# Hybrid decoder block with routed experts: whole weight rows with k outermost, and the expert's second row block in 32-row column groups in fp32

## What is computed

```
logits = xt @ w_router + b_router;  top_vals, top_idx = top_k(logits, 4);  gates = softmax(top_vals)
gu  = xb @ w_gu[e] + b_gu[e]        # w_gu[e]: 1024 x 2048
g   = min(gu[:, :1024], 7);  up = clip(gu[:, 1024:], -7, 7)
y   = ((up + 1) * g * sigmoid(1.702 * g)) @ w_down[e] + b_down[e]    # w_down[e]: 1024 x 1024
out[token] += gate * y              # then a last RMSNorm
```

## Time and profile before

| | |
|---|---|
| median of 3 runs | 2089.41 us (2071.77, 2089.41, 2090.12) |
| the profiled execution's own time | 2077.45 us |
| its span (first to last instruction) | 2075.6 us |
| PE busy | 1865.6 us, 90% |
| PE weight loads | 1518.2 us, 73% |
| DVE busy | 1480.6 us, 71% |
| ACT busy | 1143.0 us, 55% |
| POOL busy | 414.7 us, 20% |
| one split of a 1 MB piece on ACT (L1217), mean of 384 | 1.915 us |
| a weight DMA of 512 KB, issue to landing, median of 512 | 5.3 us |
| granted TensorE clock, mean | 0.948 of full |
| memory traffic | 234 GB/s over the span |

### The profile page before, as it was taken

How to read it: one execution, slowest core, us unless ns; L and a number is a source line. 1 busy time by engine, 2 the same in 40 slices (tenths; PEclk the granted TensorE clock), 3 DMA queues, 4 the chain that set the end, 5 groups by cost and what they waited for, 6 DMA issues and landing times. The chain is left out here.

```text
span 2075.6 us, 31035 instructions
## 1 busy us (share of the span) xinstructions
PE 1865.6 (90%) x8487; PEld 1518.2 (73%) x8488; DVE 1480.6 (71%) x1705; ACT 1143.0 (55%) x1262; POOL 414.7 (20%) x375
## 2 busy tenths in 40 slices
PE   6998799549999899999999999999999999999992
PEld 5776578437778787777787777777878777787772
DVE  6578525457787777888877887778777677677673
ACT  5243534155575656777756775557555455554453
POOL 4332212331111211121112211112121113112210
PEclk9999889769999999999999999999999999999996
DMA  7110213568798787999978999679879769667765
GB/s 258 31 41 1 92 61 113 121 212 264 221 350 288 252 281 253 353 358 348 342 251 278 343 356 291 219 223 350 275 247 286 223 202 317 209 227 218 228 207 182
DMA packets 348150, 486.36 MB, mean 234 GB/s; under 512 B 21512, under 2 KB 296010, under 8 KB 348112
## 3 DMA queue, kind: packets, MB, share of 16 engines
q1 hardware_dynamic: 329104, 442.03, 63.6%
q0 software_dynamic: 18864, 43.31, 8.9%
q10 hardware_dynamic: 144, 0.52, 0.1%
HBM read 451.67 MB, written 34.11 MB: 234 GB/s over the span
## 5 line engine op out<-in xcount | busy, mean ns | idle before, releaser
L1338 DVE TENSOR_TENSOR w_lo<-raw_weights,w_hi 128x2048 fp32r<-128x2048 f32 x384 | 877.8, 2290 | 324.9 <-ACT w_hi L1217 324.2
L1217 ACT ACTIVATE w_hi<-raw_weights 128x2048 fp32r<-128x2048 f32 x384 | 734.8, 1915 | 307.0 <-PE ps L1506 239.1
L1506 PE MATMUL ps<-w_hi,xT 128*128 128x512 f32 x1024 | 406.3, 397 | 0.0
L1504 PE MATMUL ps<-w_hi,xT 128*128 128x512 f32 x1024 | 406.1, 397 | 0.0
L1505 PE MATMUL ps<-w_lo,xT 128*128 128x512 f32 x1024 | 405.9, 396 | 0.0
L1505 PEld LDWEIGHTS ps<-w_lo,xT 128*128 128x128 f32 x1024 | 196.6, 192 | 42.8
L1506 PEld LDWEIGHTS ps<-w_hi,xT 128*128 128x128 f32 x1024 | 196.2, 192 | 42.2
L1504 PEld LDWEIGHTS ps<-w_hi,xT 128*128 128x128 f32 x1024 | 197.2, 193 | 40.2
L1504 PE MATMUL ps<-w_hi,hT 128*128 128x512 f32 x512 | 206.3, 403 | 0.0
L1505 PE MATMUL ps<-w_lo,hT 128*128 128x512 f32 x512 | 202.9, 396 | 0.0
L1506 PE MATMUL ps<-w_hi,hT 128*128 128x512 f32 x512 | 202.5, 396 | 0.0
(11 more groups left out here) (271 smaller groups left out, 2800.0 us busy)
## 6 DMA issues: line engine op xcount, KB each, us to landing
raw_weights<-in_w_gu SPq DMA_DIRECT2D x512, 512.0 KB, 5.3
raw_weights<-in_w_down SPq DMA_DIRECT2D x256, 512.0 KB, 5.8
rows<-in_x SPq DMA_DIRECT2D x12, 512.0 KB, 5.2
w_in_sb<-in_w_in SPq DMA_DIRECT2D x12, 512.0 KB, 4.0
raw_weights<-in_w_out SPq DMA_DIRECT2D x1, 4096.0 KB, 12.6
acc_rows<-region_c SPq DMA_DIRECT2D x8, 512.0 KB
h_rows<-region_c SPq DMA_DIRECT2D x8, 512.0 KB
acc_sb<-acc_rows SPq DMA_DIRECT2D x8, 512.0 KB, 8.4
```

Of the source, the lines that this page charges most:

```text
L1217: S.activation(w_hi[:, j % SPLIT, :, :], raw[:, j % RAW, :, :], ACT.Copy).then_inc(hi_done, 1)
L1338: V.tensor_tensor(w_lo[:, j % SPLIT, :, :], raw[:, j % RAW, :, :], w_hi[:, j % SPLIT, :, :].bitcast(F32), ALU.subtract).then_inc(lo_done, 1)
L1504: T.matmul(out[:, b, :], hi, hi_w, start=False, stop=False)
L1506: last = T.matmul(out[:, b, :], lo, hi_w, start=False, stop=end)
```

## The change

The first row block keeps its arithmetic and its 144 matmuls, in another order. Pieces 0 to 7 are now whole rows: piece k is row tile k of `w_gu` (8 KB in each partition), pieces 8 to 11 are two row tiles of `w_down`, one DMA each (`load_piece`). The raw ring has 6 slots, as the rings of the parts. k is the outer loop: for k 0 to 4 PE does the 12 matmuls of a piece into four PSUM banks, and the last three k bank by bank, so that the banks end one after another. Down goes to two banks of its own.

The second row block is done in plain fp32 from the raw pieces, in groups of 32 rows: one for 129 to 160 tokens, two for 161 to 192. For each k a group takes four matmuls with 32 stationary columns, each in its own quarter of the array's columns, over 512 weights; each quarter holds another part of the output. So raw slots are also held until PE has used them (`raw_used`). For down, quarters hold even and odd k of each column half; ACT copies the even part out (`y_tail`), DVE adds the odd (`y_tail_folded`), ACT scales. ACT evicts the first block's output in one 1024-column operation.

A unit holds up to 192 tokens now. Lists and biases are loaded by one DMA more each. On POOL the first block's output is added first; then come two holds, the second for the landing of that add, and then the second block's.

```diff
-UNIT = 256
-TAIL = P // 2
-CAP = SEQ
-UNITS_PER_E = CAP // UNIT
+TAIL, TAILS = 32, 2
+UNIT = P + TAIL * TAILS
+UNITS_PER_E = -(-SEQ // UNIT)
+CAP = UNITS_PER_E * UNIT
+ROWS_ALL = E * CAP
+LISTS = ROWS_ALL // P // 3
 DUMP = P
 ROWS = SEQ + DUMP
-GU_CH, DN_CH = 4, 2
-CH = GU_CH + DN_CH
-HALFK = KT // 2
+NP = KT + KT // 2
+PIECE = 2 * FF
+QUARTER = FF // 4
 RAW = 4
-SPLIT = 6
-AHEAD = SPLIT // 2
+RING = 6
+LAST = 3
+BIAS_ROWS, PICKS = 10, 8
...
-def load_half(sp, dram, shared, expert, j):
+def load_piece(sp, dram, shared, expert, p):
 
 
     at = bass.ds(expert, 1) if not isinstance(expert, int) else slice(expert, expert + 1)
-    slot, signal = shared["raw"][:, j % RAW, :, :], shared["raw_in"][j % RAW]
-    if j < 2 * GU_CH:
-        c, h = j // 2, j % 2
-        ks = slice(h * HALFK, (h + 1) * HALFK)
+    slot, signal = shared["raw"](p % RING), shared["raw_in"][p % RING]
+    if p < KT:
         w = dram["w_gu"][0, at].rearrange("a (k p) n -> p (a k) n", p=P)
-        q = FF // GU_CH
-        for g in range(2):
-            lo = g * FF + c * q
-            sp.dma_start(slot[:, :, g * q:(g + 1) * q], w[:, ks, lo:lo + q]).then_inc(signal, 16)
+        sp.dma_start(slot.unsqueeze(1), w[:, p:p + 1, :]).then_inc(signal, 16)
     else:
+        k = 2 * (p - KT)
         w = dram["w_down"][0, at].rearrange("a (k p) n -> p (a k) n", p=P)
-        rows = slot.rearrange("p (k g) n -> p k (g n)", k=2)
-        for i in range(2):
-            k = 2 * (j - 2 * GU_CH) + i
-            sp.dma_start(rows[:, i:i + 1, :], w[:, k:k + 1, :]).then_inc(signal, 16)
+        sp.dma_start(slot.rearrange("p (k n) -> p k n", k=2), w[:, k:k + 2, :]).then_inc(signal, 16)
...
-                for j in range(RAW, RAW + NP):
-                    hold(sp, lo_done, NP * u + j - RAW + 1, held["sp"])
+                for j in range(RING, RING + NP):
+                    hold(sp, raw_used[j // RING - 1], RING * u + j % RING + 1, held["sp"])
+                    hold(sp, lo_done, NP * u + j - RING + 1, held["sp"])
                     if j < NP:
-                        load_half(sp, dram, shared, expert, j)
+                        load_piece(sp, dram, shared, expert, j)
                     else:
                         with sp.If(u + 1 < n):
-                            load_half(sp, dram, shared, after, j - NP)
+                            load_piece(sp, dram, shared, after, j - NP)
...
+                hold(pool, next_in, 32 * (u + 2), held["pool"])
+                hold(pool, xT_ready, 2 * (u + 1), held["pool"])
+                hold(pool, xT_tail_ready, u + 1, held["pool"])
+                gather(tails_next)
                 hold(pool, added, 32 * u + 32, held["pool"])
+                load_lists(this_list, this_tail, row0, this_in)
+                hold(pool, y_gated, u + 2, held["pool"])
                 pool.indirect_dma_start(
-                    out=scratch["acc"], out_offset=bass.IndirectOffsetOnAxis(ap=this_list[:, 0, 0:1], axis=0),
-                    in_=y[:, 0, :], in_offset=None, compute_op=ALU.add).then_inc(added, 16)
+                    out=scratch["acc"], out_offset=bass.IndirectOffsetOnAxis(ap=this_list[:, 0:1], axis=0),
+                    in_=y[:, :], in_offset=None, compute_op=ALU.add).then_inc(added, 16)
+                hold(pool, y_tail_gated, u + 1, held["pool"])
+                hold(pool, added, 32 * u + 48, held["pool"])
+
+                def add_rest(rows):
+                    if rows:
+                        pool.indirect_dma_start(
+                            out=scratch["acc"], out_offset=bass.IndirectOffsetOnAxis(ap=this_tail[0:rows, 0:1], axis=0),
+                            in_=y_tail[0:rows, :], in_offset=None, compute_op=ALU.add).then_inc(added, 16)
+                    else:
+                        pool.dma_start(stand_in[:, 1, :], scratch["table"][0:1, :]).then_inc(added, 16)
+                per_tails(pool, tails, lambda t: add_rest(t * TAIL))
...
+                def unit(t):
+                    for j in range(RING, NP - 1):
+                        refill(j)
...
+                    gated(1)
+                    h_hi(0)
+                    x_hi(2 * u + 2, 0)
+                    refill(NP - 1)
+                    refill(NP)
+                    h_hi(1)
+                    refill(NP + 1)
+                    x_hi(2 * u + 3, 1)
+                    refill(NP + 2)
+                    act.wait_ge(mm_done, NP * u + KT + 1)
+                    split_bias(u + 2)
+                    refill(NP + 3)
+                    x_tail_copy(u + 2, tails_next)
+                    refill(NP + 4)
+                    if t:
+                        act.wait_ge(raw_used[1], RING * (u + 1))
+                        act.wait_ge(added, 32 * u + 32)
+                        for g in range(t):
+                            for h in range(2):
+                                last = S.activation(y_tail[g * TAIL:(g + 1) * TAIL, h * HALF:(h + 1) * HALF],
+                                                    ps[2 * h * TAIL:(2 * h + 1) * TAIL, BANK_TAIL + g, :], ACT.Copy)
+                        last.then_inc(y_tail_even, 1)
+                    else:
+                        act.sem_inc(y_tail_even, 1)
+                    gate_y()
+                    refill(NP + 5)
+                    if t:
+                        act.wait_ge(y_tail_folded, u + 2)
+                        S.activation(y_tail[0:t * TAIL, :], y_tail[0:t * TAIL, :], ACT.Copy,
+                                     scale=this_tail[0:t * TAIL, 1:2].bitcast(F32)).then_inc(y_tail_gated, 1)
+                    else:
+                        act.sem_inc(y_tail_gated, 1)
...
+                def unit(t):
...
+                    product(0)
+                    h_lo(0)
+                    product(1)
+                    x_lo(2 * u + 2, 0)
+                    refill(NP - 1)
+                    h_lo(1)
+                    refill(NP)
+                    x_lo(2 * u + 3, 1)
+                    refill(NP + 1)
+                    refill(NP + 2)
+                    split_bias(u + 2)
+                    refill(NP + 3)
+                    refill(NP + 4)
+                    if t:
+                        dve.wait_ge(y_tail_even, u + 1)
+                    for g in range(t):
+                        for h in range(2):
+                            at = y_tail[g * TAIL:(g + 1) * TAIL, h * HALF:(h + 1) * HALF]
+                            last = V.tensor_tensor(at, ps[(2 * h + 1) * TAIL:(2 * h + 2) * TAIL, BANK_TAIL + g, :], at, ALU.add)
+                    if t:
+                        last.then_inc(y_tail_folded, 1)
+                    else:
+                        dve.sem_inc(y_tail_folded, 1)
+                    refill(NP + 5)
...
+                def gate_up_tail(k, t):
+
+                    piece = interleaved(raw(k % RING))
+                    for g in range(t):
+                        for q in range(4):
+                            last = T.matmul(ps[q * TAIL:(q + 1) * TAIL, BANK_TAIL + g, :].rearrange("p (a n) -> p a n", a=2),
+                                            xT_tail[:, k, g * TAIL:(g + 1) * TAIL], piece[:, :, q, :],
+                                            start=False, stop=(k == KT - 1))
+                    last.then_inc(raw_used[k // RING], 1)
+
...
+                def down_tail(p, t):
+
+                    piece = raw(p % RING).rearrange("p (k n) -> p k n", k=2)
+                    for g in range(t):
+                        for h in range(2):
+                            for e in range(2):
+                                last = T.matmul(ps[(2 * h + e) * TAIL:(2 * h + e + 1) * TAIL, BANK_TAIL + g, :],
+                                                hT_tail[:, 2 * (p - KT) + e, g, :], piece[:, e, h * HALF:(h + 1) * HALF],
+                                                start=False, stop=(p == NP - 1))
+                    last.then_inc(raw_used[1], 1)
+
+                def unit(t):
+                    pe.wait_ge(xT_lo_done, 2 * u + 2)
+                    pe.wait_ge(xT_tail_done, u + 1)
+                    for k in range(KT - LAST):
+                        pe.wait_ge(lo_done, NP * u + k + 1)
+                        for b in range(4):
+                            last = gate_up(b, k)
+                        last.then_inc(mm_done, 1)
+                        if k == 1:
+                            pe.wait_ge(bias_done, u + 1)
+                            for b in range(4):
+                                T.matmul(ps[:, b, :], pick[:, BIAS_OF[b], :], bias[:, :], start=False, stop=False)
+                            pe.wait_ge(y_tail_folded, u + 1)
+                            for g in range(t):
+                                T.matmul(ps[:, BANK_TAIL + g, :], pick[:, 6, :], bias[:, :], start=True, stop=False)
+                            if t == 0:
+                                pe.sem_inc(raw_used[1], RING)
+                                pe.sem_inc(hT_tail_ready, 1)
+                        if t and k % 2:
```

(45 more changed lines are left out.)

633 lines of the change are left out of this document (261 added, 372 removed).

## The result

The changed kernel takes 2245.9 us (median of four, 2241.1 to 2252.9); beside it the kernel before took 2089.8 (2071.8 to 2101.7). The ratio is 1.077, 95% interval 1.072 to 1.082. The sign is as forecast and the time is still inside the range (2055 to 2250), but +80 us was forecast and +156 measured. The profiled execution took 2241.1 us with a span of 2239.5; of before 2077 and 2075.6.

What follows compares the result with a forecast made beforehand. PE was taken as the bound, with 2 to 4 us of waits in a unit. Units by kind summed to 1672 us against 1592, +80; 2089 + 80, rounded, gave 2168 us, range 2055 to 2250.

Steps and rivals of the forecast that it cites:

- Part 1: Tail in fp32 column groups: four quarters side by side, 10.3 us a group; 147 us saved if nothing waits.
- Rival (c): Tail's column quarters run one after another: +345 us, 2510 us in all; chance 0.03.
- Part 2: Whole-row weight loads, 8 KB runs for 1 KB: at most 3.9 us in 19 plain units, 74 us; at least nothing.
- the sum: Unit times by kind added over the stage: 1672 us against 1592, +80.
- Rival (d): Every POOL landing is longer behind longer weight packets: 4.5 us a unit, 145 us in 32 units, 2313 us; chance 0.10.
- Part 3: New POOL wait for the add's landing delays next tokens: PE waits 6.7 us, plain unit 44.8 us against 40.3.
- The add's landing: On POOL's chain in a plain unit, the first block's add lands 8.9 us after its issue.
- the turn of the loop 2.4: On POOL's chain, 2.4 us from the stand-in to the next unit's list.
- The gather's term: End of POOL's chain: the token gather lands in 7.3 us, its stand-in half a microsecond later.
- Part 4: Raw slots held by tail rounds: plain after tail 52.8 us, tail after plain 56.5, tail after tail 60.
- the two waits that I found on paper: PE waits 2.6 us for the fold after a tail unit and 3.6 us for the hidden rows within one.
- Rival (a): POOL's chain is hidden and parts 1 and 2 give their gains: 68 us less, 2021 us; chance 0.17.

Runs made afterwards that it cites:

- e7: Number not tied to one run: changed kernel, either next-but-one list loaded ahead of the add (2198.1 us) or tail's eviction, fold and gating before the freed piece's split (2190.9 us).
- e2: Changed kernel, all waits kept, but POOL gathers the tokens of unit u + 2 in unit u: 2037.1 us, 0.975 of the kernel before.
- e9: Changed kernel with tokens gathered a unit further ahead and both edits of order on ACT and DVE: 1964.2 us, 0.940 of the kernel before.
- e6: Changed kernel with each weight piece loaded by two DMAs, gate/up in 1 KB runs: 2273.3 us, 1.089 of the kernel before.
- e12: Kernel before, with the first block's add issued first on POOL and the second's add or stand-in waiting for its landing: 2190.1 us, 1.049.
- e5: Kernel with tokens gathered a unit further ahead, plus tail's eviction, fold and first block's gating ahead of the freed piece's split: 2007.1 us, 0.966 of the kernel before.
- e8: Kernel with tokens gathered a unit further ahead, plus the tail's hidden rows ahead of piece 10 on ACT and DVE: 1987.8 us, 0.953 of the kernel before.
- e3: Changed kernel with only the one-group body, tokens beyond 160 of the two fullest experts left out: 2216.8 us, 1.063 of the kernel before.
- e4: Changed kernel with only the two-group body, two groups in all 13 tail units: 2335.0 us, 1.121 of the kernel before.

## Why the prediction was right in sign and short in size

**Part 1, four column groups: right.** The records of two rounds in the changed kernel:

```profile
1756.57 1.92 PE L1541 MATMUL ps<-raw_more,hT_tail 128*32 128x512 f32 x16
```

```profile
1756.57 0.16 PEld L1541 LDWEIGHTS ps<-raw_more,hT_tail 128*32 128x32 f32 x8 [0.35 <-issue]
1757.02 0.13 PEld L1541 LDWEIGHTS ps<-raw_more,hT_tail 128*32 128x32 f32 x4 [0.30 <-issue]
1757.45 0.13 PEld L1541 LDWEIGHTS ps<-raw_more,hT_tail 128*32 128x32 f32 x4 [0.30 <-issue]
```

Four quarters load together every 0.43 us, the time of one record of 512 columns alone, and two records make a matmul: 0.86 a round. Sixteen records take 1.92 us where one after another they would be 6.9, and in the trace of e7 the next sixteen start 1.74 us behind the first (1862.76 and 1864.50), which is 0.87 a round. Rival (c) is out. The Trainium skill ("TensorE: Matmul & The Clock Gate", Measured speedup vs the span model) states 3.07 times for four row tiles and has no row for four column tiles; by that figure two rounds would be 2.2 us (an estimate from the page's number), and this case's rows for column groups are below it: 6.9 / 1.92 = 3.6 with the start and the end counted, and in the steady part the full four.

**Part 2, whole rows: as the sum took it.** The sum starts a plain unit at PE's 36.4 us, so it gave the whole rows all that they could give. e2 and e9, where nothing else holds a plain unit, have 37.5 and 36.8. What I had not priced is that the long runs also help the chain on POOL: without them (e6) it is 1.7 us longer, and the kernel 27 us slower, or about 40 without the stall of unit 24.

**Rival (d): refuted.** The add lands in 10.4 us with 8 KB runs and in 10.7 with 1 KB, the gather in 6.0 and 7.2, and the add in e12, whose weights are untouched, in 10.0. The Trainium skill ("DMA: Bandwidth & Descriptors", Queues, rings and completion order) states that an engine drains a whole packet of one ring before it turns to the next; no run here shows that longer descriptors make the small transfers land later, and the gathers went the other way.

**Part 3, the wait on POOL: mechanism right, sum 2.1 us short a unit.** My steps from the add's issue to PE were 8.9 + 2.9 + 7.1 + 7.8 = 26.7 us. The unit shown above has 10.2 + 4.4 + 7.0 + 6.5 = 28.1, the mean of the ten plain units behind plain ones is 10.9 + 4.4 + 7.0 + 6.4 = 28.8, and the unit of e12 has 11.0 + 4.4 + 6.3 + 8.8 = 30.5. Two terms were too short. The add's landing was taken from plain units (8.9), where the tail units had 10.3 in the same rows. And "the turn of the loop 2.4" was the bracket behind an indirect DMA of 1.67 us: start to start it was 885.25 - 881.18 = 4.1 before, and is 4.4 now, since the same work runs behind a stand-in of 0.6. The gather's term was 1.4 too long. The rest of the unit was half a microsecond longer than in the sum. So the mean plain unit is 47.4 us and not 44.8, which is 26 us in ten units.

**Part 4, tail units: right in kind, short in most terms.** Hidden rows were to be 3.6 us late and were 60.4 / 13 = 4.6. Plain units behind tails came to 53.1 for 52.8. Tail units behind plain ones came to 61.1 for 56.5, or 58.9 without number 24; those behind tails to 64.3 for 60, or 60.1 without number 30. e5 and e8 bear out that the eviction stands behind the split and the hidden rows behind a held piece: the two waits that I found on paper cost 30 and 49 us once tokens are in time. But I took both as part of the change, and they are only two lines of its order.

**The step that failed: the tail units in the sum, and a term that was not in it.** Of the 84 us between forecast and profile, units counted by kind and against the forecast's list, plain units behind plain ones have 26, the first unit 6, plain behind tails 2, and the last unit 21 less, as I had let it wait for tokens of a unit that does not exist. Tail units have 71, and 56 of these sit in four units. Two of them, numbers 24 and 30, end in stalls of 11.6 and 11.0 us for instructions and are 18 and 17 us over. The loading of code was a cost that the sum put at nothing: I had not thought of it. The other two are those with a second group (13 and 8 over). My part 1 had 60 - 48.9 = 11.1 us for a second group, but the sum put such units only 5 to 5.5 us above those with one, and gave no reason; e3 and e4 have 9.1. That makes 8 of these 21 us, the stall at the end of unit 22 makes 5.9, and the rest of them stays open. e3 shows that the stalls and the missing time are not simply added: without the third body the kernel gains some 11 us beside the groups' work, while units 23 and 25 become 7 and 8 us longer.

**The rivals' other side.** Rival (a), the chain hidden, was to be 2021 us. e2 hides it and takes 2037, and with the order of ACT and DVE mended, which (a) left as it was, 1964. So the new forms of tail and weights do gain: e9's 13 tail units last 57.1 us in the mean against 63.5 before, its plain units 38.7 against 40.3. Which part is the column groups' and which the whole rows' no run separates.

## What to carry to other kernels

When a wait is put on a queue that issues DMAs, write out the chain from start to start of all that is queued behind it, through the loop's turn to the engine that needs the last of it. If it is as long as a turn of the loop, a whole turn of lead (209 us here) cures more than a shorter chain (48 us for one landing less). And an operation that waits for the last use of a buffer belongs behind everything that is ready earlier: two such changes of order, without a single instruction saved, were worth 73 us.

## What the runs showed that I had not expected

A loop with three bodies on each engine loads instructions again around the units that take the rarest one: 43 packets in place of 17, and PE stands for 5.9 to 11.7 us with nothing named but `issue`. In a kernel that waits anyway this costs some 11 us, in the tight one some 31, both worked out with 9.1 us for a second group. Such a stall can also come and go with edits that do not touch that code, as the one of unit 24 did. Four column groups of fp32 matmuls ran fully side by side. And the landing of the add is 10 to 11 us in plain units beside 8 KB and 1 KB runs alike, though it was 8.9 in the plain units of the kernel before, where the DMA share was highest (1.08); why it was shortest there stays open.
